# A hybrid decoder layer on one Trainium2 core: where the first weight sums of the projection are made, when their slices are loaded, and how often the activation table set is named

## The chip, the core and the metric

The kernel runs on one core of a Trainium2 chip. A core has TensorE (PE in the profile), VectorE (DVE), ScalarE (ACT), GpSimd (POOL) and SyncE (SP), whose queue issues nearly all transfers of this kernel, and 16 DMA engines. Each engine works through its own instructions in order and waits on semaphores for the others. The metric is the device time of one execution in microseconds (us); lower is better.

## The reference

One layer (DEPTH is 1) over 4096 tokens of width 1024:

```
mod = silu(c) @ ada_w + ada_b;  shift, scale, gate = split(mod, 3)
h = rms_norm(x, norm_pre) * (1 + scale) + shift
u = h @ w_in                                # (4096, 1024) @ (1024, 3720)
q, k, v, f_logit, z_rwkv, p_pool, g = split(u)
y_fox = forgetting attention, 8 heads of 64: q and k are RMS-normalised per head
y_rwkv = RWKV-7 recurrence, 4 heads of 64, over z_rwkv;  y_pool = causal pooling over p_pool
y = concat(y_fox, y_rwkv, y_pool) * silu(g)
out = x + gate * rms_norm(y @ w_out, norm_post)
```

The change touches only the way to u: the preparation (norms of the rows of w_in, shift and scale) and the projection h @ w_in.

## The kernel before, in words

The program is a row of blocks, `prepare`, `project`, `recur`, `attend` and `output`, with a barrier of all engines between one and the next. The change is in the first two.

**prepare** streams the eight row groups of w_in (128 x 3720 fp32 each, L143) and of the first 2048 columns of ada_w (L148) through SP's queue, in the order of the code: the four first loads, then w_in and ada_w by turns, each gated by the use of the slot it goes to. DVE takes the largest absolute value of each row of w_in (L257), and after the eighth makes its inverse `rinv` (L276). PE multiplies the ada_w slices by silu(c) (L221, 16 small matmuls a slice). Behind the w_in and ada_w loads SP issues eight loads of x (L165, the first 512 tokens in four tiles of two halves), and behind those the slices of w_in that the projection needs first: a wide one of 128 columns (L167) and a narrow one of 8 columns (L168, runs of 32 bytes) into slot 1 of `wraw`, and two of 128 columns (L171, `columns[0]`) into slot 0. ACT squares the x tiles and makes their inverse norms with Ln and Exp (L205 to L210); DVE scales the tiles (L248, `x_scaled`). A short chain of DVE (L279 to L285) makes a bound over all columns, POOL reduces it over the partitions (L194), and DVE makes the scales from it (L288 to L293). ACT names the table set that holds both Ln and Exp once here (L201).

**project** splits each fp32 operand into two fp16 pieces, high and low, and multiplies by a Strassen-like scheme with seven products of half-size blocks, so sums and differences of blocks have to be made of both operands. The token side runs over 4 super-blocks (`sb_`) of 1024 tokens, the weight side over 14 sets of 2 x 128 columns (`n`, `q` = n - 1 in super-block 0) and one single of 128 + 8 columns (n = 0). A step `g` is one of the 7 products of a set, or the single.

Before the loop over g stands a first phase, which makes the token side of super-block 0 in 16 units `u`: PE transposes (L676, `turn`), ACT brings the four blocks over (L722, L723), DVE makes four sums (L903 to L908), ACT rounds to the high pieces (L739), DVE subtracts for the low pieces (L915, `low`; semaphore `lo_made`). PE runs the single in four parts (`single(0, j)`, L652 and L659, L661), the j-th when 4(j + 1) units are low and `single_low` is done; in PE's order part j stands ahead of the transposes of unit 4(j + 2). DVE runs `single_low` (L926 to L931) at u = 6 and the low pieces of set 0 (L940 to L951) at u = 14 and 15. POOL begins with `single_weights` (L1117 to L1124: scale by rinv, high pieces, one difference), then `weight_sums(0)` (L1131 to L1143: scale 128 x 2048 by rinv, then four 128 x 512 differences), `first_high` (L1148 to L1151), and then the passes of `weight_sums(q)` for q = 1, 2, ... of the loop. SP loads the slices of set 1 (L507) when `single_low` is done, those of set 2 when the low pieces of set 0 are.

In the loop, a set of q or k columns needs per-head norms. For the x-th such tile: ACT squares it (L798), PE sums the squares with a matmul against `headmean` into the one bank `pss` (L684, `head_means`), ACT takes Ln of that bank (L804) and Exp (L806), DVE multiplies (L979, `normalise`), POOL rounds and stores. `head_means(x)` waits for the square of x and for the Ln of x - 1, since the bank is one; PE's next products are queued behind it. The square of x waits for `normalise(x - 2)`. There are 64 such tiles, 16 in a super-block, 4 in a set; the q and k sets are n = 7, 9, 11 and 13. Ahead of every Ln of L804 stands `preload_act_table_set(EXP_LN)` (L803), and so ahead of every Ln of `squares` (L748; 12 times, for the x tiles of the next super-block). The Sigmoid of the gate columns (L837, n = 1 to 4) is in another set.

## Time and profile before

| | us |
|---|---|
| three timed runs | 3635.66, 3657.88, 3661.07 |
| their median | 3657.88 |
| the profiled execution's own time | 3640.25 |
| its span in the trace | 3638.5 |
| PE busy in the span | 3315.0 (91%) |

The trace is of the execution of 3640.25 us, of which 1.75 us lie outside the span. Times in the rows below are counted from the span's start. `prepare` lasts until PE's first transposes at 82.4 us; the first phase of `project` from there to about 157 us; the loop of `project` to about 1430 us. A busy share of PE near 9 tenths or more means that whatever makes PE wait lengthens the time; idle time of the other engines costs only what it hands on to PE.

### The profile page before, as it was taken

What the parts mean: (1) busy time and instruction counts of PE and PEld (TensorE: products, weight loads), DVE (VectorE), ACT (ScalarE), POOL (GpSimd) and SP (SyncE); (2) the same over time, 40 slices, a digit from 0 to 9 for tenths busy, and PEclk for the clock granted to TensorE, in tenths of its full rate; (3) what the DMA queues carried; (4) which work ended last, traced back from release to release, by engine and by line L of the source; (5) the groups of instructions that cost most, each with busy time, mean ns of one, the idle gap of its engine ahead of it and who ended that gap; (6) DMA issues with size and microseconds to landing.
All of it is one profiled execution on the core that took longest, in us unless ns stands there. A gap on an engine that the chain in (4) does not pass through costs nothing. (4 is left out here: it accounts for less than half of the span.)

```text
span 3638.5 us, 90159 instructions
## 1 busy us (share of the span) xinstructions
PE 3315.0 (91%) x31941; PEld 2290.6 (63%) x31941; DVE 2435.1 (67%) x4320; ACT 2048.2 (56%) x3785; POOL 1793.2 (49%) x2071
## 2 busy tenths in 40 slices
PE   6597899999999997699999699999999999979998
PEld 6593369449647943588888366666666656645444
DVE  5797556434532333688784599889988988965554
ACT  2344654544543244577775477777777777753333
POOL 1477300330140042245553398889889889862222
PEclk9798999999999999799998699999999999989999
DMA  8297335334443533233221222020220211214555
GB/s 326 72 307 283 125 133 188 128 133 155 152 154 120 187 136 123 55 81 81 63 56 35 56 56 55 10 58 12 54 57 10 56 33 32 57 69 162 189 187 183
DMA packets 251932, 402.69 MB, mean 111 GB/s; under 512 B 86733, under 2 KB 203172, under 8 KB 236612
## 3 DMA queue, kind: packets, MB, share of 16 engines
q1 hardware_dynamic: 251019, 396.89, 34.6%
q8 instruction: 258, 4.23, 0.5%
q14 instruction: 175, 1.43, 0.1%
q0 software_dynamic: 480, 0.14, 0.1%
HBM read 274.38 MB, written 122.59 MB: 109 GB/s over the span
## 5 line engine op out<-in xcount | busy, mean ns | idle before, releaser
L2526 ACT ACTIVATE p<-psc,xb,sc 128x512 f32<-128x512 f32 (+3 forms) x1152 | 848.7, 744 | 318.4 <-PE psc L2617 305.7
L2504 POOL TENSOR_TENSOR plo<-p 128x512 f16<-128x512 f32 (+2 forms) x864 | 905.5, 1076 | 71.9 <-ACT p L2526 70.8
L2673 DVE TENSOR_REDUCE mx<-pm 128x1 f32<-128x512 f32 (+3 forms) x1201 | 732.0, 636 | 99.4 <-PE pm L2548 87.0
L627 PE MATMUL bank<-h,ring 128*128 128x512 f16 x2688 | 605.1, 384 | 5.4 <-DVE u L963 5.4
L2596 PE MATMUL po<-v,p 128*128 128x129 f16 x4224 | 513.3, 220 | 21.2 <-POOL plo L2504 18.0
L632 PE MATMUL bank<-ring,h 128*128 128x128 f16 x8064 | 465.7, 221 | 24.1 <-ACT c L791 12.3
L2598 PE MATMUL po<-v,plo 128*128 128x65 f16 x4224 | 483.7, 192 | 3.5 <-issue 3.5
L627 PEld LDWEIGHTS bank<-h,ring 128*128 128x128 f16 x2688 | 265.8, 99 | 350.5 <-issue 52.9
L632 PEld LDWEIGHTS bank<-ring,h 128*128 128x128 f16 x8064 | 462.9, 99 | 25.0 <-issue 12.6
L2596 PEld LDWEIGHTS po<-v,p 128*128 128x128 bf16 x4224 | 388.8, 97 | 123.7 <-POOL plo L2504 28.0
L1158 POOL CAST stage<-c 128x512 f16<-128x512 f32 x64 | 47.3, 740 | 814.1 <-DVE c L979 814.1
L2548 PE MATMUL pm<-ka,qa 128*128 128x512 f16 (+3 forms) x1201 | 438.4, 368 | 3.2 <-DVE mx L2673 2.8
L2598 PEld LDWEIGHTS po<-v,plo 128*128 128x128 f16 x4224 | 379.2, 98 | 95.9
L2615 PE MATMUL psc<-qa,ka 128*128 128x512 f16 (+3 forms) x1152 | 420.1, 365 | 0.0
L2617 PE MATMUL psc<-qb,kb 128*128 128x512 f16 (+3 forms) x1152 | 418.5, 363 | 0.0
L2889 PE MATMUL pz<-wo,yh 128*128 128x512 f16 x1024 | 305.9, 380 | 3.1 <-DVE yl L2921 3.1
L973 DVE TENSOR_TENSOR c<-bank,u 128x512 f32<-128x512 f32 x168 | 115.5, 688 | 249.6 <-PE bank L627 170.7
L2717 DVE TENSOR_TENSOR plo<-p 128x512 f16<-128x512 f32 (+1 forms) x288 | 281.6, 978 | 0.0
L2833 POOL TENSOR_TENSOR o<-o,xr 128x1024 f32<-128x1024 f32 x32 | 75.4, 2356 | 312.1 <-DVE o L2944 312.1
L2548 PEld LDWEIGHTS pm<-ka,qa 128*128 128x128 f16 x1201 | 118.6, 99 | 133.9 <-DVE mx L2673 14.6
L2889 PE MATMUL pz<-wo,yl 128*128 128x512 f16 x512 | 194.6, 380 | 0.0
L2889 PEld LDWEIGHTS pz<-wo,yh 128*128 128x128 f16 x1024 | 100.4, 98 | 117.7 <-issue 4.9
(405 smaller groups left out, 5662.3 us busy)
## 6 DMA issues: line engine op xcount, KB each, us to landing
ring<-scratch_ws SPq DMA_DIRECT2D x52, 1792.0 KB, 7.8
scratch_z<-stage SPq DMA_DIRECT2D x72, 256.0 KB, 2.8
scratch_ws<-h SPq DMA_DIRECT2D x10, 1792.0 KB, 8.1
y<-scratch_y SPq DMA_DIRECT2D x35, 512.0 KB
g<-scratch_g SPq DMA_DIRECT2D x35, 512.0 KB
xr<-in_x SPq DMA_DIRECT2D x34, 512.0 KB, 6.3
scratch_g<-stage SPq DMA_DIRECT2D x64, 256.0 KB, 5.9
scratch_qk<-stage SPq DMA_DIRECT2D x64, 256.0 KB, 2.6
```

The lines of the kernel that those rows point to most:

```text
L627: t = nc.tensor.matmul(bank[b][:], m.ring[:, slot, l, bo, k, :], hh[:, side, r, ao, k, :], start=fresh and first, stop=last, skip_group_ch ...
L632: t = nc.tensor.matmul(bank[b][:, ts], hh[:, side, l, ao, k, ts], m.ring[:, slot, r, bo, k, :], start=fresh and first and tp == 0, stop=la ...
L2504: nc.gpsimd.tensor_tensor(plo[:, k % NP, 0:w], p32[:, k % NP, 0:w], hi[:, 0:w], ALU.subtract)\
L2526: nc.scalar.activation(p32[:, k % NP, 0:w], psc[k % 2][:, 0:w], ACT.Exp, bias=xb[:, u, b, x // 4:x // 4 + 1], scale=m.sc[:, 0:1]).then_inc ...
L2548: ins = nc.tensor.matmul(pm[g][:, n, 0:w], qa[:, u, j * P:(j + 1) * P], ka[:, u, q * BT:q * BT + w], start=not last, stop=True, skip_group ...
L2596: nc.tensor.matmul(o[:, oc:oc + VW], hi[:, c0:c0 + P], v[:, u, x, 0:VW], start=(x == 0 and t % 2 == 0), stop=False, skip_group_check=True)
L2598: g = nc.tensor.matmul(o[:, oc:oc + 1 + HD], plo[:, k % NP, c0:c0 + P], v[:, u, x, 0:1 + HD], start=False, stop=(x == 4 * b + t), skip_gro ...
L2615: nc.tensor.matmul(psc[k % 2][:, 0:w], ka[:, u, ks], qa[:, u, t0:t0 + w], start=not diag, stop=False, skip_group_check=diag)
L2617: nc.tensor.matmul(psc[k % 2][:, 0:w], kb[:, u, ks], qb[:, u, t0:t0 + w], start=False, stop=True, skip_group_check=diag).then_inc(qk_mm.se ...
L2673: nc.vector.tensor_reduce(mx[:, s, t, q:q + 1], pm[g][:, 0, 0:w], AX.X, ALU.max).then_inc(pm_d.sem, 1)
L2717: tt(plo[:, k % NP, 0:w], p32[:, k % NP, 0:w], hi[:, 0:w], ALU.subtract).then_inc(lo_v.sem, 1)
L2889: mm = nc.tensor.matmul(pz[u % 2][j][:], l[:, u % 2, k // 4, ks], r[:, k, j * HALF:(j + 1) * HALF], start=(k == 0 and c == 0), stop=(k == ...
```

## The change

In `prepare`, SP issues the wide, the narrow and the two `columns[0]` slices right behind the first two pairs of w_in and ada_w, ahead of the loads with k = 2. POOL does there what `single_weights` and `weight_sums(0)` did in `project`: as soon as rinv is there (a new semaphore, `inverse`) it makes the single's scaled slice, its difference and its high pieces, then comes the reduction over partitions, then the scaling and the four differences of set 0. The difference of the single goes to a place of its own (`m.wtz`), and `wz` and `wf` live from `prepare` on. In `project`, POOL begins with `first_high`. Sets 0 and 1 now share one buffer of sums (`wt_of`), so the differences of set 1 wait until the low pieces of set 0 are made (`w_lo` of 2); `single_low` moves from u = 6 to u = 3, the low pieces of set 0 from u = 14 and 15 to u = 9 and 12. The table set is named ahead of L804 only at the first tile of each super-block, and in `squares` only from the third super-block on (`sb_ > 1`): 4 and 8 times in the code where it was 64 and 12.

```diff
--- before.py
+++ after.py
@@ -156,6 +156,13 @@
                 load_w(0)
                 load_ada(1)
                 load_w(1)
+                wide = slice(Z_COL + 6 * P, Z_COL + 7 * P)
+                sp.dma_start(m.wraw[:, 1, :, 0:P], a.w_in[0, :, wide].rearrange("(k p) c -> p k c", p=P)).then_inc(m.wraw_in[1], 16)
+                sp.dma_start(m.wraw[:, 1, :, P:P + FOX_HEADS], a.w_in[0, :, F_COL:F_COL + FOX_HEADS]
+                             .rearrange("(k p) c -> p k c", p=P), allow_slow_non_contiguous=True).then_inc(m.wraw_in[1], 16)
+                for side, c0 in enumerate(m.columns[0]):
+                    sp.dma_start(m.wraw[:, 0, :, side * P:(side + 1) * P], a.w_in[0, :, c0:c0 + P].rearrange("(k p) c -> p k c", p=P))\
+                        .then_inc(m.wraw_in[0], 16)
                 for k in range(2, KT):
                     load_w(k)
                     load_ada(k)
@@ -163,13 +170,6 @@
                     for half in range(2):
                         t0 = half * BT + j * P
                         sp.dma_start(m.x_first[j][:, half, :], a.x[0, t0:t0 + P, :]).then_inc(m.x_in[j], 16)
-                wide = slice(Z_COL + 6 * P, Z_COL + 7 * P)
-                sp.dma_start(m.wraw[:, 1, :, 0:P], a.w_in[0, :, wide].rearrange("(k p) c -> p k c", p=P)).then_inc(m.wraw_in[1], 16)
-                sp.dma_start(m.wraw[:, 1, :, P:P + FOX_HEADS], a.w_in[0, :, F_COL:F_COL + FOX_HEADS]
-                             .rearrange("(k p) c -> p k c", p=P), allow_slow_non_contiguous=True).then_inc(m.wraw_in[1], 16)
-                for side, c0 in enumerate(m.columns[0]):
-                    sp.dma_start(m.wraw[:, 0, :, side * P:(side + 1) * P], a.w_in[0, :, c0:c0 + P].rearrange("(k p) c -> p k c", p=P))\
-                        .then_inc(m.wraw_in[0], 16)
 
             @block.gpsimd
             def _(pool):
@@ -190,8 +190,31 @@
                 for k in range(ZC // P):
                     pool.dma_start(m.Z[k * P:(k + 1) * P, 0:m.HALO], zero[:]).then_inc(halo, 16)
 
+                tt, copy, wz, wf, wtz = nc.gpsimd.tensor_tensor, nc.gpsimd.tensor_copy, m.wz, m.wf, m.wtz
+                r, w = m.wraw[:, 1, :, :], P + FOX_HEADS
+                pool.wait_ge(m.wraw_in[1], 32)
+                pool.wait_ge(inverse, 1)
+                tt(r[:, :, 0:w], r[:, :, 0:w], m.rinv[:].unsqueeze(2).to_broadcast([P, KT, w]), ALU.mult).then_inc(wz_step, 1)
+                pool.wait_ge(wz_step, 1)
+                tt(wtz, r[:, 4:8, 0:w], r[:, 0:4, 0:w], ALU.subtract).then_inc(wz_step, 1)
+                copy(wz[:, 0, 0:2, :, :].rearrange("p o k c -> p (o k) c"), r[:, :, 0:P])
+                copy(wf[:, 0:2, :, 0:FOX_HEADS].rearrange("p o k c -> p (o k) c"), r[:, :, P:w])
+                pool.wait_ge(wz_step, 2)
+                copy(wz[:, 0, 2, :, :], wtz[:, :, 0:P])
+                copy(wf[:, 2, :, 0:FOX_HEADS], wtz[:, :, P:w])
                 pool.wait_ge(w_max, KT + 1)
                 nc.gpsimd.partition_all_reduce(bnd[:, 1:2], bnd[:, 0:1], P, RMAX).then_inc(allmax, 1)
+                r, t = m.wraw[:, 0, :, :], m.wt
+                pool.wait_ge(m.wraw_in[0], 32)
+                tt(r, r, m.rinv[:].unsqueeze(2).to_broadcast([P, KT, 2 * P]), ALU.mult).then_inc(wq_step, 1)
+                b11, b12, b21, b22 = r[:, 0:4, 0:P], r[:, 0:4, P:2 * P], r[:, 4:8, 0:P], r[:, 4:8, P:2 * P]
+                pool.wait_ge(wq_step, 1)
+                tt(t[:, 0, :, :], b12, b11, ALU.subtract).then_inc(wq_step, 1)
+                tt(t[:, 2, :, :], b22, b12, ALU.subtract).then_inc(wq_step, 1)
+                pool.wait_ge(wq_step, 2)
+                tt(t[:, 1, :, :], b22, t[:, 0, :, :], ALU.subtract).then_inc(wq_step, 1)
+                pool.wait_ge(wq_step, 4)
+                tt(t[:, 3, :, :], b21, t[:, 1, :, :], ALU.subtract).then_inc(wq_step, 1)
                 pool.wait_ge(halo, 16 * (ZC // P))
 
             @block.scalar
@@ -273,7 +296,7 @@
 
                 dve.wait_ge(w_max, KT)
                 chain(nc.vector.tensor_scalar(rowmax[:], rowmax[:], 1e-20, 1.0 / TW, ALU.max, ALU.mult))
-                chain(nc.vector.reciprocal(rinv[:], rowmax[:]))
+                nc.vector.reciprocal(rinv[:], rowmax[:]).then_inc(inverse, 1)
                 x_scaled(0)
                 dve.wait_ge(ada_mm, KT)
                 chain(nc.vector.tensor_tensor(m.ab[:], pcol[:, 0:2 * KT], m.cols[:, KT:3 * KT], ALU.add))
...
@@ -345,7 +367,6 @@
         hh = m.h
         wraw, wout = m.wraw, m.wout
         wts = [m.wt, m.xt[:].rearrange("p s d -> p (s d)").rearrange("p (o k c) -> p o k c", o=4, k=4)]
-        wtz = m.wt.rearrange("p o k c -> p (o k c)")[:, 0:4 * (P + FOX_HEADS)].rearrange("p (k c) -> p k c", k=4)
         early = c[:].rearrange("p n t -> p (n t)").rearrange("p (s o t) -> p s o t", s=2, o=8)
         acc = h7[:].rearrange("p s o t -> p (s o t)")[:, 0:DM]
         ones = h7[:].rearrange("p s o t -> p (s o t)")[:, DM:DM + P]
@@ -488,6 +509,9 @@
             if u >= 4:
                 eng.wait_ge(lo_made, u - (3 if u < 16 else 1))
 
+        def wt_of(q):
+            return wts[0] if q <= 0 or q % 2 else wts[1]
+
         def slot_of(q):
             return (m.ring if q < DIRECT else wout)[:, q % 2, :, :, :, :]
 
@@ -501,7 +525,7 @@
                     elif q == 2:
                         sp.wait_ge(w_lo, 2)
                     else:
-                        sp.wait_ge(w_sums, q)
+                        sp.wait_ge(w_sums, q - 2)
                         sp.wait_ge(w_lo_a, q - 2)
                     for side, c0 in enumerate(m.columns[q]):
                         sp.dma_start(wraw[:, q % 2, :, side * P:(side + 1) * P], a.w_in[0, :, c0:c0 + P].rearrange("(k p) c -> p k c", p=P))\
+                        nc.scalar.preload_act_table_set(EXP_LN)
                     activate(m.rstd[:, j, :], m.ssq[:, j, :], ACT.Ln, bias=m.eps[:, 0:1], scale=1.0 / DM).then_inc(std_x, 1)
                     act.wait_ge(std_x, nth_ + 1)
                     activate(m.rstd[:, j, :], m.rstd[:, j, :], ACT.Exp, scale=-0.5).then_inc(rstd_x, 1)
 
                 def weights_high_a(q):
 
-                    act.wait_ge(w_step, 1 + q * 4 + 1)
+                    act.wait_ge(w_step, 4 * (q - 1) + 1)
                     if 2 <= q < DIRECT:
                         act.wait_ge(mm, ended(0, q - 1, NP7 - 1))
                     if q == DIRECT:
@@ -765,8 +790,8 @@
 
                 def weights_high_b(q):
 
-                    act.wait_ge(w_sums, q + 2)
-                    activate(slot_of(q)[:, 0, 3:7, :, :], wts[(q + 1) % 2], ACT.Copy).then_inc(w_hi, 1)
+                    act.wait_ge(w_sums, q)
+                    activate(slot_of(q)[:, 0, 3:7, :, :], wt_of(q), ACT.Copy).then_inc(w_hi, 1)
 
                 def first_product(sb_, n):
 
@@ -800,7 +825,8 @@
                 def head_inverse(x):
 
                     act.wait_ge(ss_d, x + 1)
-                    nc.scalar.preload_act_table_set(EXP_LN)
+                    if x % 16 == 0:
+                        nc.scalar.preload_act_table_set(EXP_LN)
                     activate(sq[:, x % 2, :], pss[:], ACT.Ln, bias=m.eps[:, 0:1]).then_inc(ln_d, 1)
                     act.wait_ge(ln_d, x + 1)
                     activate(sq[:, x % 2, :], sq[:, x % 2, :], ACT.Exp, scale=-0.5).then_inc(rec_d, 1)
...
@@ -922,7 +948,6 @@
                 def single_low():
 
                     r = wraw[:, 1, :, :]
-                    dve.wait_ge(w_first_hi, 1)
                     tt(wz[:, 1, 0:2, :, :].rearrange("p o k c -> p (o k) c"), r[:, :, 0:P],
...
@@ -933,7 +958,7 @@
                 def weights_low_a(q):
 
                     if q == 0:
-                        dve.wait_ge(w_first_hi, 2)
+                        dve.wait_ge(w_first_hi, 1)
                     else:
                         dve.wait_ge(w_hi, 2 * q - 1)
                     h, o, r = slot_of(q)[:, 0], slot_of(q)[:, 1], wraw[:, q % 2, :, :]
@@ -948,7 +973,7 @@
                     if q >= 1:
                         dve.wait_ge(w_hi, 2 * q)
                     h, o = slot_of(q)[:, 0], slot_of(q)[:, 1]
-                    tt(o[:, 3:7, :, :], wts[(q + 1) % 2], h[:, 3:7, :, :], ALU.subtract).then_inc(w_lo, 1)
+                    tt(o[:, 3:7, :, :], wt_of(q), h[:, 3:7, :, :], ALU.subtract).then_inc(w_lo, 1)
 
                 def first_sum(sb_, n):
 
@@ -1041,13 +1066,13 @@
                 for u in range(18):
                     if u < 16:
                         sums(u)
-                    if u == 6:
+                    if u == 3:
                         single_low()
                     if u >= 2:
                         low(u - 2)
-                    if u == 14:
+                    if u == 9:
                         weights_low_a(0)
-                    if u == 15:
+                    if u == 12:
                         weights_low_b(0)
                 dve.wait_ge(fb_in, 16)
                 dve.wait_ge(carry0, 2)
@@ -1110,30 +1135,16 @@
                     ins.then_inc(pool_step, 1)
                     pool.wait_ge(pool_step, steps[0])
 
-                def single_weights():
-
-                    r, w, copy = wraw[:, 1, :, :], P + FOX_HEADS, nc.gpsimd.tensor_copy
-                    pool.wait_ge(m.wraw_in[1], 32)
-                    tt(r[:, :, 0:w], r[:, :, 0:w], m.rinv[:].unsqueeze(2).to_broadcast([P, KT, w]), ALU.mult).then_inc(w_step, 1)
-                    pool.wait_ge(w_step, 1)
-                    copy(wz[:, 0, 0:2, :, :].rearrange("p o k c -> p (o k) c"), r[:, :, 0:P])
-                    copy(wf[:, 0:2, :, 0:FOX_HEADS].rearrange("p o k c -> p (o k) c"), r[:, :, P:w])
-                    tt(wtz[:, :, 0:w], r[:, 4:8, 0:w], r[:, 0:4, 0:w], ALU.subtract).then_inc(w_sums, 1)
-                    pool.wait_ge(w_sums, 1)
-                    copy(wz[:, 0, 2, :, :], wtz[:, :, 0:P])
-                    copy(wf[:, 2, :, 0:FOX_HEADS], wtz[:, :, P:w]).then_inc(w_first_hi, 1)
-
                 def weight_sums(q):
 
-                    r, t = wraw[:, q % 2, :, :], wts[(q + 1) % 2]
-                    done = 1 + q * 4
+                    r, t = wraw[:, q % 2, :, :], wt_of(q)
+                    done = 4 * (q - 1)
                     pool.wait_ge(m.wraw_in[q % 2], 32 * (q // 2 + 1) + (32 if q % 2 else 0))
                     tt(r, r, m.rinv[:].unsqueeze(2).to_broadcast([P, KT, 2 * P]), ALU.mult).then_inc(w_step, 1)
                     b11, b12, b21, b22 = r[:, 0:4, 0:P], r[:, 0:4, P:2 * P], r[:, 4:8, 0:P], r[:, 4:8, P:2 * P]
                     pool.wait_ge(w_step, done + 1)
-                    if q:
-                        pool.wait_ge(w_lo, q)
-                    else:
+                    pool.wait_ge(w_lo, max(q, 2))
+                    if q == 2:
                         pool.wait_ge(tr_d, 4)
                     tt(t[:, 0, :, :], b12, b11, ALU.subtract).then_inc(w_step, 1)
                     tt(t[:, 2, :, :], b22, b12, ALU.subtract).then_inc(w_step, 1)
@@ -1147,8 +1158,7 @@
                     o, r, copy = m.ring[:, 0, 0, :, :, :], wraw[:, 0, :, :], nc.gpsimd.tensor_copy
                     copy(o[:, 0:2, :, :].rearrange("p o k c -> p (o k) c"), r[:, :, 0:P])
                     copy(o[:, 2, :, :], r[:, 4:8, P:2 * P])
-                    pool.wait_ge(w_sums, 2)
-                    copy(o[:, 3:7, :, :], wts[1]).then_inc(w_first_hi, 1)
+                    copy(o[:, 3:7, :, :], wts[0]).then_inc(w_first_hi, 1)
 
                 def pieces(sb_, n, half, side):
                     t, x = tile(sb_, n, half, side), nth(sb_, n, half, side)
@@ -1182,8 +1192,6 @@
                     step(tt(stage[hi, s, 0:BT], stage[hi, s, 0:BT], ps4[hi, m.HALO:E], ALU.add))
                     pool.sem_inc(ready[s], 1)
 
-                single_weights()
-                weight_sums(0)
                 first_high()
                 nc.gpsimd.memset(ph[:], 0.0).then_inc(p_clear, 1)
                 pool.wait_ge(p_clear, 1)
@@ -3001,6 +3009,8 @@
             m.h = weights.enter_context(nc.sbuf_tensor("h", [P, 2, 2, 7, 4, BT], F16))
             m.ring = weights.enter_context(nc.sbuf_tensor("ring", [P, 2, 2, 7, 4, P], F16))
             m.xt = weights.enter_context(nc.sbuf_tensor("xt", [P, 2, DM], F32))
+            m.wz = weights.enter_context(nc.sbuf_tensor("wz", [P, 2, 3, 4, P], F16))
+            m.wf = weights.enter_context(nc.sbuf_tensor("wf", [P, 3, 4, 2 * FOX_HEADS], F16))
             m.pscale = weights.enter_context(nc.sbuf_tensor("pscale", [P, 2], F32))
             m.rtab = weights.enter_context(nc.sbuf_tensor("rtab", [P, 2, m.HALO], F32))
             m.ssq = weights.enter_context(nc.sbuf_tensor("ssq", [P, 4, 2], F32))
@@ -3009,6 +3019,7 @@
             m.wraw = other[:, 0:4096].rearrange("p (s k c) -> p s k c", s=2, k=KT)
             m.wt = other[:, 4096:6144].rearrange("p (o k c) -> p o k c", o=4, k=4)
             m.wout = other[:, 6144:13312].bitcast(F16).rearrange("p (s l o k c) -> p s l o k c", s=2, l=2, o=7, k=4)
+            m.wtz = other[:, 12288:12288 + 4 * (P + FOX_HEADS)].rearrange("p (k c) -> p k c", k=4)
             m.x_first = [m.xt] + [other[:, 6144 + j * 2 * DM:6144 + (j + 1) * 2 * DM].rearrange("p (s d) -> p s d", s=2)
                                   for j in range(3)]
             prepare(nc, a, m)
```

## Rows read from the trace of the kernel before

**Rows 1.** The page, busy time, share of the span and instructions of each engine.

```profile
PE 3315.0 (91%) x31941; PEld 2290.6 (63%) x31941; DVE 2435.1 (67%) x4320; ACT 2048.2 (56%) x3785; POOL 1793.2 (49%) x2071
```

**Rows 2.** Windows: start:end, length, busy time per engine, PE clock, DMA share, GB/s.

```profile
0.00:82.40 82.40, 56.21 (x258) 55.43 (x258) 43.99 (x56) 13.63 (x27) 9.55 (x24) 1.00 0.93 360
82.40:157.00 74.60, 32.86 (x384) 29.41 (x384) 58.95 (x93) 29.82 (x50) 32.08 (x21) 0.70 0.11 29
```

**Rows 3.** Waits of PE, 156 to 1500 us: us in total, times, longest.

```profile
PE pss L684 <- ACT sq L804: 48.6, 28, 6.4
...
PE ptr L676 <- DVE xt L920: 7.9, 1, 7.9
```

**Rows 4.** The three lines that name the set: duration min/median/max in ns, first to last.

```profile
L803 ACT ACT_TABLE_LOAD  x64: 1283/1283/1283, 312.2 to 1414.6; - x64
...
L748 ACT ACT_TABLE_LOAD  x12: 1283/1283/1283, 358.1 to 951.1; - x12
...
L201 ACT ACT_TABLE_LOAD  x1: 1283/1283/1283, 4.8 to 4.8; - x1
```

**Rows 5.** Timeline in a late q or k set: start, us, operation [idle before <-releaser].

```profile
1405.91 0.72 ACT L798 ACTIVATE sq<-c,sc 128x512 f32<-128x512 f32 x1 [1.40 <-DVE c L979]
...
1406.65 1.28 ACT L803 ACT_TABLE_LOAD   x1
...
1407.94 0.69 ACT L804 ACTIVATE sq<-pss,eps 128x512 f32<-128x512 f32 x1
...
1408.78 1.10 PE L684 MATMUL pss<-sq,headmean 128*128 128x512 f32 x2 [0.90 <-ACT sq L804]
...
1413.52 1.10 PE L684 MATMUL pss<-sq,headmean 128*128 128x512 f32 x2 [1.06 <-ACT sq L804]
```

**Rows 6.** Timeline, other head waits of PE, and what ran around them.

```profile
432.44 1.10 PE L684 MATMUL pss<-sq,headmean 128*128 128x512 f32 x2 [0.90 <-ACT sq L804]
...
436.80 1.28 ACT L748 ACT_TABLE_LOAD   x1
...
441.26 2.05 PE L684 MATMUL pss<-sq,headmean 128*128 128x512 f32 x2 [5.13 <-ACT sq L804]
...
669.38 1.71 PE L684 MATMUL pss<-sq,headmean 128*128 128x512 f32 x2 [3.40 <-ACT sq L804]
...
670.88 3.88 PE L627 MATMUL bank<-h,ring 128*128 128x512 f16 x12
...
716.65 1.10 PE L684 MATMUL pss<-sq,headmean 128*128 128x512 f32 x2 [1.06 <-ACT sq L804]
```

**Rows 7.** Timeline at the end of the preparation.

```profile
58.66 14.12 PE L221 MATMUL pcol<-ccol,adaw 128*128 128x1 f32 x64 [0.48 <-DMA adaw<-in_ada_w]
...
63.01 9.76 SPq L168 DMA_DIRECT2D h<-in_w_in  x1
...
68.32 1.06 ACT L205 ACTIVATE sqp<-xt 128x1024 bf16<-128x1024 f32 x1 [62.25 <-DMA xt<-in_x]
...
74.31 0.38 POOL L194 PARTITION_ALL_REDUCE bnd<-bnd  x1 [64.23 <-DVE bnd L285]
...
79.59 1.42 DVE L248 TENSOR_SCALAR h<-h,rstd 128x1024 f32<-128x1024 f32 x2 [0.76 <-ACT rstd L210]
```

**Rows 8.** Timeline in the first phase of the projection.

```profile
96.92 3.68 DVE L903 TENSOR_TENSOR h<-h 128x128 f32<-128x128 f32 x1
...
118.58 3.60 POOL L1131 TENSOR_TENSOR h<-h,rinv 128x2048 f32<-128x2048 f32 x1 [8.41 <-DMA h<-in_w_in]
...
126.27 1.99 POOL L1143 TENSOR_TENSOR h<-h 128x512 f32<-128x512 f32 x1
...
130.99 1.08 DVE L915 TENSOR_TENSOR h<-h 128x896 f16<-128x896 f32 x1
...
132.92 1.08 DVE L915 TENSOR_TENSOR h<-h 128x896 f16<-128x896 f32 x1
...
150.96 4.44 PE L652 MATMUL bank<-h,wz 128*128 128x128 f16 x48 [4.79 <-DVE h L915]
```

More of the change, by code:

```diff
@@ L131, in prepare @@
         x_sq, x_std, x_rstd = sem("p_x_sq"), sem("p_x_std"), sem("p_x_rstd")
-        tab_made = sem("p_tab_made")
+        tab_made, inverse, wz_step, wq_step = sem("p_tab_made"), sem("p_inverse"), sem("p_wz_step"), sem("p_wq_step")
         zero = sb("zero", [P, m.HALO])
```

5 lines of the change are left out of this document (2 added, 3 removed).

## The prediction

> **What bounds the kernel now.** I read the page's first part, then windows by stage, then PE's own waits, then the timeline at the places those named. PE is busy 91% of the span [rows 1], so work taken off another engine counts only where PE waits for it. Two stretches are different: up to 82.4 us the DMA engines carry the time (share 0.93, 360 GB/s), and from 82.4 to 157 us PE is busy 32.86 of 74.60 us at a granted clock of 0.70, while DVE is busy 58.95 us [rows 2]. That first phase is bound by DVE, much of whose busy time is waiting for POOL, as shown below. In the loop of the projection the largest wait of PE is for the Ln of the head norms, 28 times, 48.6 us together, and one wait for scaled x adds 7.9 us [rows 3].
>
> **Part 1, the table set.** The three lines that name it give 64, 12 and 1 loads of 1283 ns each [rows 4]. The single naming in the preparation serves four tiles of Square, Ln and Exp (there is one load at L201, none beside it), so a set once there stays. The change leaves 4 of 64 and 8 of 12: 60 + 4 loads go, 64 x 1.283 = 82 us of ScalarE. What counts is their share of PE's waits. In a late set the square starts at 1405.91 and takes 0.72, the load follows at 1406.65, the Ln at 1407.94, and PE goes on at 1408.78 after 0.90 of idleness, and again at 1413.52 after 1.06 [rows 5]. The load stands in both chains, and it is longer than each wait, so each vanishes whole. Ten waits are of 0.90 (first 432.44, last 1408.78) and ten of 1.06 (first 716.65, last 1413.52) [rows 5, 6]: 9.0 + 10.6 = 19.6 us. The other eight make 48.6 - 19.6 = 29.0 us, from 2.10 to 6.39; each holds one removed load (1.28), and that of 5.13 at 441.26 also one of L748 at 436.80 [rows 6], where both go: 7 x 1.28 + 2.57 = 11.5 us. The wait for scaled x [rows 3] has one load of L748 ahead of it: 1.3 us. Sum 32.4 us. Could the chains meet a new stop at once? Behind the first wait of a set of q or k lies the same chain again (Exp, normalise, square, Ln), and it moves up by the same 1.28, so the second gain is not paid for by the first. Of the rest of each long wait, DVE's order of work is the cause, and it stays.
>
> After the waits of 3.40 and 5.13 the pss pair took 1.71 and 2.05, after the short ones 1.10, and behind the first twelve matmuls took 3.88 [rows 6]. PE had stood idle, and went on slower. If those twelve lose in the same ratio, such a place costs 0.61 + 3.88 x (1 - 1.10 / 1.71) = 2.0 us. With waits of 2.1 in place of 3.4 some of it may go; I take it for three places at half, 3 us (bounds 0 and 7). Table part: 35 us, bounds 28 and 40.
>
> The Trainium skill (ScalarE: Activation LUTs, What ACT_TABLE_LOAD costs) adds to the load a drain of about 1.38 us at a switch to a different set. By it the eight long waits would give 9 x 1.38 = 12 us more. The trace differs: the load starts 0.02 us after the square's end and the Ln right behind it [rows 5], so I leave it out of the sum.
>
> **Part 2, the preparation.** Four transfers move ahead of the k = 2 loads. They carry 0.52 + 0.03 + 1.05 = 1.6 MB, 4.5 us at 360 GB/s [rows 2]. SP was held 9.76 us at the narrow one, with a full queue in front [rows 7]; the same can happen now, and queued behind it are w_in 2, ada_w 2 and all that follows. While SP is held, the DMA engines have what fills the queue, so I count bytes and a little for the narrow runs: 5 us, bounds 3 and 10. Everything behind shifts: PE's eight passes over ada_w (14.12 for two, the last ending at 72.8), x (ACT begins its squares at 68.32) and the reduction over partitions at 74.31 [rows 7], now near 79.3. What the wait for bytes at the tail gives back is small, since the squares, not the trailing slices, ended the block.
>
> POOL's single part (one scaling, one difference, copies, some 5.5 us by width from the 3.60 of the 2048-wide scaling [rows 8]) fits between the inverse, near 72, and the reduction: hidden. The part of set 0 does not. A pass takes from 118.58 to 128.26, 9.7 us [rows 8], so it ends near 89.6. Meanwhile DVE has its three scales and six x_scaled halves (1.42 a pair [rows 7]) to do. Are they held up by POOL? A sum of 0.28 us became 3.68 while POOL scaled [rows 8]; these are other forms, so the bounds are 0 and all of them after POOL, 4.3 + 0.6 for the last small ones. I take half, 2 us: the block ends near 92 instead of 82.4, **9.6 us later**, bounds 6 and 15. The Trainium skill (SBUF — State Buffer, Who interferes with whom) says that a tensor_scalar in a two-port mode, and any operation with two inputs in SBUF, blocks against GpSimd for a whole instruction. By it I would take the upper end, 12 us. It speaks against doing this here.
>
> **Part 3, the first phase.** S is its start. Free of POOL a unit takes DVE 132.92 - 130.99 = 1.93 us [rows 8], about 0.93 for the sums and 1.0 for the low pieces. During a pass of POOL, 9.7 us, about one operation of DVE gets in at each of POOL's five boundaries (the 3.68 at 96.92 is one held until POOL's scaling ended), some 2.7 us of work; loss 7. Before, POOL's passes for sets 0 and 1 and the copies fall on DVE's way, single_low waits for POOL, and the last part of the single starts at 150.96, S + 68.6 [rows 8]. After, step by step: the copies of first_high hold DVE until S + 3.8; four units low with two sums ahead (9.6) and single_low between (1632 wide, by the 1.08 for 896 about 1.9) give S + 15. PE's first part takes 4.44 and its small matmuls (5.5, an estimate); the transposes for unit 8 are queued behind it, so with ACT's moves DVE has the next sums at S + 22.5. POOL's scaling for set 1 (its slices issued at S + 10, landing some 6 later by estimate) falls into this stall. Eight units are low at S + 26.3, the second part runs and holds unit 12 until S + 33.5, and DVE makes the low pieces of set 0 (3584 wide, 4 by the same rate) by S + 37.5. Now `w_lo` is 2, which frees POOL's four differences of set 1, 6 us, and SP's loads of set 2, which by the same 6 us land just as those end (near S + 44): a whole second pass follows without a gap, until S + 54. DVE has three groups of sums and five lows to do, 7.8 us, and is caught in both. Twelve units are low at S + 44, sixteen at S + 57.8, where the last part of the single starts. That is 92 + 57.8 = 149.8 against 150.96: **1.2 us sooner**. Bounds: 12 sooner (DVE slips more through POOL's gaps) and 12 later (preparation at its upper end, nothing slipping). The two thirds of POOL's work that left the first phase are paid for by the preparation, and the new wait on `w_lo` brings two passes together at the end of the chain. Later sets keep their order against PE.
>
> **The sum.** -35 - 1 = -36 us, from the profiled execution's own time 3640.25 (span 3638.5 and 1.75 outside): 3604. The median of the runs is 3657.88, and two of three lie near 3660, so the same change from there gives 3622. I can't tell on which level the middle run falls, and take 3614.
>
> **The rivals.**
> - The first phase gains and the preparation loses little: front -12, total -47, 3593 to 3611. For it: DVE's stalls on PE leave slack. Chance 0.12.
> - The preparation costs its upper end: front +12, total -24, 3616 to 3634. For it: the 9.76 us of SP and the 3.68 of a blocked sum. Chance 0.15.
> - The load was not what PE waited for, and normalise or the square's wait takes its place: only the pairs of 0.90 and 1.06 half, total -10, 3630 to 3648. Against it the timeline, in which Ln follows the load at once. Chance 0.05.
> - Slower than before: without the name ahead of each Ln, Ln and Exp are given sets of their own, two loads a tile in place of one. Then Exp, normalise and the next square come 1.28 later at all 28 waits: 28 x 1.28 = 36 us more, 3640 + 36 = 3676 (3694 from the median). It decides as soon as a load stands ahead of L806. Against it: one load at L201 for four pairs of Ln and Exp [rows 4]. Chance 0.03.
> - The skill's drain, by which a removed load frees 2.66: 12 us more than my sum, 3592 to 3610. The gap of 0.02 speaks against it. Chance 0.02.
>
> The forecast itself has 0.63, with its own range of 3597 to 3632.
>
> **How the numbers follow.** From 3590 (low level, front at its best) to 3642 (high level, front at its worst or a third of the table part lost) no more than 0.2 is left out. About 1% is what a measurement of this kernel can tell from no change, here 36.6 us, that is 3621. The forecast sits just on the good side when the middle run falls low and on the line when it falls high; with the better cases faster by over 1% gets 0.54, within 1% 0.43, slower by over 1% 0.03.
>
> **What would show it.** Right: L803 x4 and L748 x8; the row of PE waiting for L804 down to some 17 us in 8 waits, with none of 0.90 or 1.06; PE's first transposes near 92; the reduction near 79; L903 rows of several us only at S to S + 4, near S + 17 and from S + 37 on; the last start of L652 near 150. Wrong: loads in front of Exp; a new releaser in the place of L804; transposes past 97 (SP's queue starved the loads) or before 88; a last part of the single before 140 or after 160.

## The result, and the profile after

The changed kernel takes 3614.3 us in the median of 8 runs (3603.77 to 3624.66), the kernel before 3655.85 in 8 runs on the same chip (3635.66 to 3664.90). The ratio is 0.9891, with a 95% interval of 0.9866 to 0.9915: 41.5 us less by the medians. The interval does not reach 1, so the change is faster; whether by more than 1% it leaves open, since 0.9900 lies inside it. The forecast of 3614 met the time. Its two parts did not: the table part gave about 12 us more than forecast and the front took about 12 us more, and the two misses cancelled.

The page of the changed kernel, busy time of each engine (before: [rows 1]):

```profile
PE 3329.5 (92%) x31941; PEld 2311.4 (64%) x31941; DVE 2425.5 (67%) x4320; ACT 1963.3 (54%) x3721; POOL 1791.5 (49%) x2071
```

The two lines that name the set in the loop, by source line (columns as in [rows 4]):

```profile
L829 ACT ACT_TABLE_LOAD  x4: 1283/1283/1283, 324.0 to 1248.5; - x4
...
L773 ACT ACT_TABLE_LOAD  x8: 1283/1283/1283, 532.9 to 936.1; - x8
```

PE's waits between 156 and 1500 us (in total, times, longest, as in [rows 3]):

```profile
PE pss L708 <- ACT sq L830: 14.3, 8, 4.7
...
PE ptr L700 <- DVE xt L946: 6.7, 1, 6.7
```

ScalarE has 64 instructions less, exactly the loads, and 85 us less, of which the loads are 82. The wait for Ln [rows 3] fell from 48.6 us in 28 waits to 14.3 in 8. TensorE's matmuls are the same 31941.

The stages of the changed kernel, by windows (columns as in [rows 2]). The first two answer to the two of [rows 2]:

```profile
0.00:104.50 104.50, 56.22 (x257) 55.39 (x258) 44.19 (x56) 13.63 (x27) 24.25 (x35) 1.00 0.74 284
104.50:168.40 63.90, 34.55 (x384) 31.15 (x384) 54.82 (x93) 29.94 (x50) 23.66 (x14) 0.71 0.13 34
1392.00:2194.00 802.00, 705.33 (x6220) 580.05 (x6219) 575.04 (x1128) 516.07 (x1431) 393.24 (x469) 0.86 0.24 61
```

The preparation ends at 104.5 instead of 82.4 us and moves 284 GB/s instead of 360. The first phase, from there to the first product of the loop, is 10.7 us shorter. The third window is code that the change leaves alone. In the same stretch behind the projection the kernel before has this row:

```profile
1428.00:2230.00 802.00, 704.42 (x6495) 575.87 (x6495) 598.47 (x1166) 534.32 (x1460) 414.73 (x498) 0.89 0.24 61
```

PE is as busy in both, but finishes 6220 matmuls instead of 6495, at a granted clock of 0.86 instead of 0.89. What follows the projection takes 2231.3 us in the trace of after (3622.9 - 1391.6), 2211.1 in that of before and 2213.9 in that of the kernel with the table part alone (below, clock 0.90 in this stretch). The source there is the same in all three. So the spans of two single executions (3622.9 and 3638.5) understate the change. I therefore compare two things: medians, and **the end of the projection**, the first matmul behind its loop:

```profile
L733 PE MATMUL ptr<-h x4: 592/592/592, 1391.6 to 1392.9; 128*128 128x512 f32 x4
```

In before it starts at 1427.4. That is 35.8 us sooner, as the traces have it:

| kernel | first transposes | last part of the single | first product of the loop | end of the projection |
|---|---|---|---|---|
| before | 82.4 | 150.96 | 157.50 | 1427.4 |
| after | 104.5 | 161.93 | 168.91 | 1391.6 |
| tables_only | 82.3 | 150.86 | 157.44 | 1379.7 |
| front_only | 103.3 | 160.52 | 167.18 | 1437.0 |
| pe_reduce | 94.4 | 151.98 | 159.12 | 1382.0 |
| loads_early | 89.5 | 158.18 | 164.77 | 1434.7 |
| loads_late | 107.7 | 165.37 | 172.71 | 1395.9 |
| tables_pe_reduce | 82.3 | 148.34 | 154.73 | 1373.5 |
| own_sums | 95.6 | 148.58 | 156.00 | 1379.5 |
| single_sooner | 82.4 | 145.68 | 152.52 | 1375.0 |

These are single executions. Kernels with the same preparation differ by up to 1.2 us in its end (after and front_only, pe_reduce and own_sums), so a difference of about that size between two rows shows nothing.

From before to after the first product comes 11.4 us later, and from there to the end of the projection 47.2 us are gained. Two questions followed: why the tables give 47 and not 35, and where 22 us come from in a preparation that was to lose 9.6.

### The profile page after: what moved, and what is told of

It is laid out like the page before. It is cut to its first block and busy times, and to the rows that moved or that the text cites. A ratio compares the mean times of both kernels' runs of the same rounds, so it can differ in the third digit from the quotient of the medians.

```text
span 3622.9 us, 90094 instructions
## 1 busy us (share of the span) xinstructions
PE 3329.5 (92%) x31941; PEld 2311.4 (64%) x31941; DVE 2425.5 (67%) x4320; ACT 1963.3 (54%) x3721; POOL 1791.5 (49%) x2071
```

## The experiments

**1. The two parts apart.** tables_only is the kernel before with the two conditions on the table set and nothing else; front_only is the changed kernel with the set named each time.

```diff
+                    if sb_ > 1:
+                        nc.scalar.preload_act_table_set(EXP_LN)
...
+                    if x % 16 == 0:
+                        nc.scalar.preload_act_table_set(EXP_LN)
```

> The kernel before with nothing but the table set named less often (4 and 8 times instead of 64 and 12). Theory: the table part alone carries the gain, and the front part costs some 11 us. Then the preparation and the first phase stay as before (first transposes at 82.4, last part of the single at 151), each later super-block takes 301 us instead of 310, and the projection's last matmuls start near 1380 instead of 1427: 47 us less, ratio 0.987, and some 11 us faster than the changed kernel. Rival: the first super-block's extra gain (18 us where 10 were forecast) comes from GpSimd being ahead with the weight sums; then the last matmuls start near 1388 and the ratio is 0.990.

> The changed kernel with the table set named as often as before (64 and 12 times), so only the front part is left. Theory: 11 us slower than before, ratio 1.003; first transposes at 104.5, last part of the single at 162, the 28 waits of PE for the Ln of the head norms there as before with 48 us, last matmuls of the projection near 1439. Rival: the sums that are made ahead shorten the first super-block by some 8 us; then they start near 1431 and the time is within 3 us of before.

Measured: tables_only 3608.09 us (5 runs) against 3652.79 (17 runs of before), ratio 0.9873 (0.9842 to 0.9903), end of the projection 47.7 sooner. front_only 3665.88 (12 runs), ratio 1.0040 (1.0019 to 1.0060), end of the projection 9.6 later. So the tables carry the whole gain, and the front is a small loss. (The intervals of after and tables_only overlap; that tables_only is the better of the two rests on the front's own loss in front_only and on the end of the projection, 11.9 sooner.) The rival that POOL's work, now done sooner, helps the first super-block fell: that super-block is 18.3 us shorter with the tables alone (from the first product to the start of the second super-block, 364.64 to 346.35), and 18.0 in after.

**2. Who makes the reduction over partitions.** In after POOL stands still around it. The timeline of the changed kernel at the end of the preparation:

```profile
80.48 0.21 POOL L204 CAST wf<-h 128x32 f16<-128x32 f32 x1
...
81.38 0.16 DVE L308 TENSOR_TENSOR bnd<-bnd 128x1 f32<-128x1 f32 x1
...
86.35 0.38 POOL L206 PARTITION_ALL_REDUCE bnd<-bnd  x1 [5.66 <-issue]
...
88.13 4.07 DVE L271 TENSOR_SCALAR h<-h,rstd 128x1024 f32<-128x1024 f32 x6
...
93.64 3.59 POOL L209 TENSOR_TENSOR h<-h,rinv 128x2048 f32<-128x2048 f32 x1 [6.91 <-issue]
...
101.09 1.26 POOL L217 TENSOR_TENSOR h<-h 128x512 f32<-128x512 f32 x1
...
104.53 1.94 PE L700 MATMUL ptr<-ident,xt 128*128 128x128 f32 x8 [24.54 <-PEq L74]
```

POOL is free at 80.69 and its input is there at 81.54, but the reduction starts at 86.35. The next scaling, whose slices landed long before, starts 6.91 behind it. In neither gap does the profile show anything that POOL waits for. The gap ahead of the reduction is counted from POOL's last operation and not from the input: in loads_late (experiment 3) the bound is ready at 74.30, 9 us before POOL's last copy ends, and the gap behind that copy is 5.58 all the same. pe_reduce takes the reduction from POOL: PE turns the bounds into a row, DVE takes the maximum, PE spreads it over the partitions.

```diff
-                pool.wait_ge(w_max, KT + 1)
-                nc.gpsimd.partition_all_reduce(bnd[:, 1:2], bnd[:, 0:1], P, RMAX).then_inc(allmax, 1)
+                pe.wait_ge(w_max, KT + 1)
+                nc.tensor.transpose(prow[0:1, :], bnd[:, 0:1], m.ident[:]).then_inc(allmax, 1)
+                pe.wait_ge(allmax, 2)
+                nc.tensor.matmul(pall[:, 0:1], mrow[0:1, 0:P], mrow[0:1, P:P + 1], start=True, stop=True).then_inc(allmax, 1)
...
+                nc.vector.tensor_reduce(mrow[0:1, P:P + 1], prow[0:1, :], AX.X, ALU.max).then_inc(allmax, 1)
```

> The changed kernel, with the maximum over the partitions made by a transpose on PE, a maximum on DVE and a one-row matmul instead of partition_all_reduce on GpSimd. Theory: the idle 5.7 us ahead of that operation and 6.9 us behind it are the price of GpSimd changing over to other code and back, and both lie on the way to the end of the preparation. Then GpSimd goes on with set 0 at 81 to 82 without a gap, the first transposes start at 93 instead of 104.5, and the time is 11 us below the changed kernel: ratio to before 0.986. Rival: the gaps are waits for the bound and for DVE's scaling; then set 0 starts after 86 and the gain is under 3 us.

> The kernel before with the tables of the change and with the reduction on PE, nothing moved. In the kernel before GpSimd stood idle for 15 us between the reduction and the single's weights, 7.3 of them after the barrier. Theory: that too is the change of code; GpSimd starts at 82.5 instead of 89.7, the single's weights and the first low pieces come 7 us sooner, the last part of the single starts near 144 instead of 151, and the time is 7 us below tables_only, near 0.985. Rival: the first phase is held by DVE alone, and an earlier GpSimd only moves its collisions; then it is within 2 us of tables_only.

Measured: pe_reduce 3609.39 us (6 runs), ratio 0.9872 (0.9839 to 0.9904). Its first transposes start at 94.4 instead of 104.5, and the projection ends 9.6 sooner than in after. Its timeline:

```profile
78.44 0.67 POOL L206 CAST wf<-h 128x32 f16<-128x32 f32 x1
79.08 4.09 POOL L209 TENSOR_TENSOR h<-h,rinv 128x2048 f32<-128x2048 f32 x1
...
79.83 3.36 DVE L308 SCALAR_TENSOR_TENSOR gcol<-ab,cols 128x8 f32<-128x8 f32 x1
...
85.81 0.37 PE L248 MATMUL prow<-ident,bnd 128*1 128x128 f32 x1 [6.23 <-DVE bnd L313]
...
94.38 1.94 PE L707 MATMUL ptr<-ident,xt 128*128 128x128 f32 x8 [7.24 <-PEq L74]
```

Both gaps are gone: the scaling follows the copy at once. What the gaps had covered now shows. A sum of eight columns (L308) takes 3.36 us, until POOL's scaling is done, where the like one (L303) took 0.31 in after. With the next sums it brings the bound to 85.76 instead of 81.54. POOL's pass is over at 88.30, and the preparation now ends with DVE's six halves of x and four small scales, at 93.51: DVE is last where POOL was. That is why 11.7 us of lateness removed (4.8 ahead of the reduction, 6.9 behind it) gave 10.1, and 8.9 in own_sums, whose preparation is the same (95.6). The first scale of DVE is taken from `pall`, the reduction's new place.

The kernel before has such a gap too: its first scaling in the projection, in the timeline, is

```profile
89.74 1.99 POOL L1117 TENSOR_TENSOR h<-h,rinv 128x1088 f32<-128x1088 f32 x1 [15.05 <-issue]
```

It starts 7.3 us after the engines have met at 82.4. tables_pe_reduce (tables_only with the reduction on PE) removes it, with the slices loaded as before, so the gap was no wait for them. Its timeline:

```profile
82.33 2.01 POOL L1126 TENSOR_TENSOR h<-h,rinv 128x1088 f32<-128x1088 f32 x1 [72.25 <-POOLq L74]
...
148.34 4.28 PE L659 MATMUL bank<-h,wz 128*128 128x128 f16 x48 [3.67 <-DVE h L924]
```

POOL starts 7.4 sooner, but the last part of the single only 2.5 sooner (148.34 against 150.86). That DVE meets the same work of POOL elsewhere is my reading; no run takes it apart. The end of the projection is 6.2 sooner than in tables_only, 3.5 of it gained behind the first product: PE's two rows of waiting for DVE's u add 10.4 and 4.0 us there, 11.9 and 5.5 in tables_only. The time is 3600.16 us (5 runs), ratio 0.9863 (0.9831 to 0.9894), the lowest median of all. Both expectations, that the work moves up by the length of the gap, held for POOL, and only in part for PE.

**3. The place of the loads.** loads_early is the kernel before with the four slice loads moved ahead of the loads with k = 2, and nothing else. loads_late is the changed kernel with them back behind the loads of x.

```diff
@@ loads_late, on the changed kernel
-                wide = slice(Z_COL + 6 * P, Z_COL + 7 * P)
...
                 for k in range(2, KT):
                     load_w(k)
                     load_ada(k)
...
+                wide = slice(Z_COL + 6 * P, Z_COL + 7 * P)
```

> The kernel before, with only the four slices loaded amid w_in as in the changed kernel. Theory: the place of the loads alone puts ada_w, w_in and x 7 us later, since SP stands at the narrow slice (11 us in the changed kernel) with the k = 2 loads queued behind it. Then PE's last pass over ada_w ends at 80 instead of 72.8, the first transposes start near 89.6, the last part of the single near 158, and the time is 7 us above before, ratio 1.002. Rival: the bytes alone count, 4.5 us at 360 GB/s, and what trails at the end before is saved; then the transposes start at 85 to 87.

> The changed kernel, with the four slices loaded behind x as before. Theory: GpSimd's work in the preparation then waits for them: single's weights from 78, the reduction at 90, set 0 from 97 to 106, first transposes near 108 although PE's passes over ada_w end at 72.8 again. Some 3 to 4 us slower than the changed kernel, ratio 0.990. Rival: the 7 us that the loads cost come back whole; then the transposes start at 98.

Measured: loads_early 3661.03 us (10 runs) against 3656.23 (17 runs of before), ratio 1.0017 (0.9993 to 1.0040). Its first transposes start at 89.5 and its projection ends at 1434.7, 7.1 and 7.3 later. By the times alone it can't be told from before (the interval holds 1); the 7 us are the traces'. loads_late 3621.94 (4 runs), ratio 0.9911 (0.9888 to 0.9934); first transposes at 107.7, end of the projection 1395.9, 4.3 later than in after. The timeline of the changed kernel shows how it comes:

```profile
5.79 11.27 SPq L161 DMA_DIRECT2D h<-in_w_in  x1
17.10 6.59 SPq L164 DMA_DIRECT2D h<-in_w_in  x2
...
24.36 0.61 SPq L148 DMA_DIRECT2D adaw<-in_ada_w  x1
...
35.64 6.99 PE L244 MATMUL pcol<-ccol,adaw 128*128 128x1 f32 x32 [10.78 <-DMA adaw<-in_ada_w]
...
73.00 6.99 PE L244 MATMUL pcol<-ccol,adaw 128*128 128x1 f32 x32 [0.65 <-DMA adaw<-in_ada_w]
```

SP is held 17.9 us by the slices, so the load of ada_w 2 is issued only at 24.36. In before it is issued at 17.63, when its slot comes free, so 6.7 of the 17.9 delay it. PE, which multiplies ada_w as it comes, stands 10.78 us (4.46 in before), and its last pass ends at 80.0 instead of 72.8. That is 7.2 us. So the early place costs 7.2 by itself, and loads_early shows it (7.1) without any of POOL's part. In loads_late that price is gone (PE's last pass ends at 72.9), but POOL's part for the single stands ahead of the reduction in its queue and waits for slices that are now the last to land, so the reduction itself comes at 89.04 instead of 86.35. The timeline of loads_late:

```profile
89.04 0.38 POOL L206 PARTITION_ALL_REDUCE bnd<-bnd  x1 [5.58 <-issue]
...
96.84 3.59 POOL L209 TENSOR_TENSOR h<-h,rinv 128x2048 f32<-128x2048 f32 x1 [7.42 <-issue]
```

Given that POOL's work stays in the preparation, the early place was the better one by the traces; the intervals of the two times overlap. Two more gaps of 5.58 and 7.42 us stand around the reduction here.

**4. Can the moved work be made to pay?** own_sums is pe_reduce with a buffer of its own for the sums of set 1, so that POOL need not wait for the low pieces of set 0. single_sooner is tables_pe_reduce with `single_low` at u = 3.

```diff
@@ own_sums, on pe_reduce
+            return m.wt1 if q == 1 else wts[0] if q <= 0 or q % 2 else wts[1]
...
-                    pool.wait_ge(w_lo, max(q, 2))
+                    if q == 1:
+                        pool.wait_ge(tr_d, 8)
+                    else:
+                        pool.wait_ge(w_lo, q)
@@ single_sooner, on tables_pe_reduce
-                    if u == 6:
+                    if u == 3:
```

> pe_reduce, and the sums of set 1 go to a place of their own (the space of the first x tile behind xt), so GpSimd's differences for set 1 wait for eight transposes instead of the low pieces of set 0. Theory: that wait is what brings two passes of GpSimd together at the end of the first phase, where VectorE is the chain; without it the pass for set 1 runs at once behind its scaling, at 110 to 120, half of it while VectorE waits for PE anyway, and the last part of the single starts at 144 to 147 instead of 152. Ratio 0.985. Rival: VectorE loses the same at either place; then it stays at 151 to 153.

> tables_pe_reduce, and VectorE makes the single's low pieces at u = 3 instead of u = 6. GpSimd has the single's high pieces ready at 88 there, so nothing waits. Theory: the first part of the single starts when four units are low, near 105 instead of 110, SP's loads of set 1 start sooner by as much, and the last part of the single starts near 145 instead of 148.3: 3 us below tables_pe_reduce. Rival: the collisions with GpSimd only move, and the last part stays within 1 us.

Measured: own_sums 3604.71 us (6 runs), ratio 0.9864 (0.9838 to 0.9891). single_sooner 3603.28 (5 runs), ratio 0.9865 (0.9845 to 0.9886). The last part of the single starts at 148.58 in own_sums, 53.0 behind the first transposes instead of 57.6: the wait on `w_lo` had cost 4.6 us. The projection ends 2.5 sooner; of the rest, 1.2 is the later end of the preparation in this execution. In single_sooner it starts at 145.68, 2.7 sooner as expected, and the projection still ends 1.5 later than without the move: PE's two rows of waiting for DVE's u add 12.0 and 5.4 us in place of 10.4 and 4.0. Those rows are 11.9 and 5.5 in tables_only too, so it is tables_pe_reduce that has them short, and why is open. By the end of the projection no move of the front beats the tables with the reduction on PE. By their times tables_only, pe_reduce, tables_pe_reduce, own_sums and single_sooner (0.9863 to 0.9873) can't be told apart.

## Why the prediction was right, and what in it was wrong

**The table part: mechanism right, size low (35 forecast, 47.7 measured).** PE's waits for Ln, square and scaled x, 60.0 us together in before (48.6 + 3.5 + 7.9), are 22.3 in tables_only (14.8 + 0.8 + 6.7). That is 37.7 where I had 32.4. Nineteen of the twenty waits of 0.90 and 1.06 vanished; that of 0.90 at 432.44 became 0.65 (at 422.77). The eight long ones gave 14.9 where I had 11.5, since two chains held two loads where I counted one: in the first super-block 3.40 became 0.69 (at 381.06, then 377.43), and 2.56 vanished. 5.13 became 2.42, two loads as I had counted. A wait of 3.52 for the square, which I had at nothing, became 0.85.

```profile
377.43 1.10 PE L684 MATMUL pss<-sq,headmean 128*128 128x512 f32 x2 [0.69 <-ACT sq L806]
...
1355.57 1.02 PE L684 MATMUL pss<-sq,headmean 128*128 128x512 f32 x2
...
1359.02 1.02 PE L684 MATMUL pss<-sq,headmean 128*128 128x512 f32 x2
```

This is the timeline of tables_only, at that place and in a late set. It also shows a part of the remaining 10.0 us. From one pss pair to the next it is 3.45 us where no wait is left. With a wait of 1.06 in [rows 5] it was 4.74, that is 1.29 more: a short wait costs some 0.23 us beyond its idle time. Over the nineteen that went this makes 4.3.

The larger part is the slow restart, a term I had at 3 us. At five places of before, behind waits of 3.52 (422.69), 5.13 (441.26), 2.56 (484.50) and twice 3.40 (669.38 and 979.77), the step from the start of the pss pair to that of the next group is 1.7, 1.6, 1.7, 1.5 and 1.5 us longer than at the same place of tables_only, 7.9 together. One of them, in the timeline of before:

```profile
979.77 1.49 PE L684 MATMUL pss<-sq,headmean 128*128 128x512 f32 x2 [3.40 <-ACT sq L804]
...
981.05 4.09 PE L627 MATMUL bank<-h,ring 128*128 128x512 f16 x12
```

And the place at 669.38, in the timeline of the changed kernel, where the twelve matmuls now take 2.75 us:

```profile
662.39 1.10 PE L708 MATMUL pss<-sq,headmean 128*128 128x512 f32 x2 [1.98 <-ACT sq L830]
```

What fell at such a place is the granted clock. The windows of before (columns as in [rows 2]), the first two at 484.50 and the last at 381.06:

```profile
484.50:490.10 5.60, 5.60 (x18) 2.40 (x19) 0.75 (x1) 4.66 (x7) 1.77 (x2) 0.70 0.26 89
486.40:488.40 2.00, 2.00 (x6) 0.66 (x5) 0.00 (x0) 1.98 (x3) 1.24 (x2) 0.50 0.00 0
381.00:385.00 4.00, 3.94 (x18) 1.97 (x18) 2.19 (x6) 1.55 (x3) 0.55 (x1) 1.00 0.00 0
```

It fell to 0.50, the lower of its two levels (1.2 GHz), for part of the stretch; over the five places it is 0.67 to 0.70, and at all five it is 1.00 in tables_only. The length of the wait alone does not decide it: behind the 3.40 at 381.06 the clock stayed at 1.00 and the twelve took 2.75. I had taken the restart at three places and at half, since the wait would remain; the runs show five, and that behind what is left of the waits (1.97 and 2.42) PE goes on at full pace. 7.9 and 4.3 make 12.2; the stretches between, which I did not trace one by one, take 2.2 of it back.

**The preparation: 9.6 forecast, 22.1 measured; the step that failed is the set-0 pass.** I let it follow the reduction at once. By the forecast's own chain: the bound was ready 2.2 us later than I had it (the loads cost 7.2, not 5, though within their bounds of 3 and 10), the reduction started 4.8 late, and the scaling 6.9 behind it; the pass itself was 1.0 shorter, and the rest 0.4. Together 12.5, which is the miss. In that rest two errors cancel: from the end of POOL's pass (102.35) to the first transposes it took 2.15 us, near the 2.4 that I had, but not for the reason I gave, since DVE was done 9.6 us before that end. In the three traces in which POOL is last (after, front_only, loads_late) this step is 2.15, where DVE is last some 0.9. The two gaps were not among my bounds, and 22.1 lies outside 6 to 15. The trace of before had the row: POOL stood 15.05 us before its first scaling, and only half of that was the meeting of the engines. I had read POOL's rows from 118 us on and not the first. The Trainium skill (GPSIMD Engine Reference, Instruction dispatch) tells of a load of about 6 us on the first call to a freshly loaded kernel, with no instruction in the profile; the size and the invisible gap agree with 5.66 (after, front_only) and 5.58 (loads_late) ahead of the reduction. It says nothing of a second price on the way back, 6.91, 7.58, 7.42 and 7.3 here.

**DVE blocked by POOL: my 2 us were not paid in after, but the mechanism is there.** The six halves of x took 4.07 us while POOL stood in its gap. Without the gap, in pe_reduce, a small sum was held 3.36. The rule that I weighed against the change (the Trainium skill, SBUF — State Buffer, Who interferes with whom) agrees with that row. Its price was hidden by a larger one.

**The loads.** The sign that I had named, transposes past 97 because SP's queue starved the loads, came in (104.5), and loads_early shows the queue's share of it: 7.1.

**The first phase: right, and closely.** Forecast 57.8 us from the first transposes to the last part of the single; it was 57.4. The steps stand in the timeline of the changed kernel, with the start S at 104.5:

```profile
121.30 3.69 DVE L929 TENSOR_TENSOR c<-c 128x128 f32<-128x128 f32 x1
...
142.50 1.38 POOL L1149 TENSOR_TENSOR h<-h 128x512 f32<-128x512 f32 x1 [17.66 <-DVE ring L976]
...
148.45 3.65 POOL L1143 TENSOR_TENSOR h<-h,rinv 128x2048 f32<-128x2048 f32 x1
148.56 3.69 DVE L930 TENSOR_TENSOR c<-c 128x128 f32<-128x128 f32 x1
...
161.93 4.87 PE L676 MATMUL bank<-h,wz 128*128 128x128 f16 x48 [8.45 <-DVE h L941]
```

DVE is caught once at S + 17; POOL waits for the low pieces of set 0 until S + 38; the loads of set 2 land just as its differences end, and a whole second pass follows from S + 44. Where I wrote that the two thirds of POOL's work that left are paid for by the preparation, the sign was right: the phase gained 11.2 us and the preparation lost 22.1. With the preparation at 22.1 that still gave a loss and not the gain of 1.2.

**The rivals.** That the front gains fell (it lost 11). The rival of +12 for the front came nearest to its 11.0, though not by its own working: it had the preparation at its upper end of 15, and that took 22.1. Its total of -24 fell with the tables. Three others fell: that the load was not what PE waited for, that Ln and Exp get sets of their own (no load stands ahead of Exp: 4 and 8 loads in all), and a drain at each load. The last needs a word, since 47.7 is near the 47 that it gave. The rule of the Trainium skill (ScalarE: Activation LUTs, What ACT_TABLE_LOAD costs) is for a switch to a different set, and the removed loads named the set that was there, since no other load came in their place. Whole waits vanished at late sets for one load and nothing more: 1.29 from pair to pair is the wait and its restart, and a drain of 1.38 ahead of a load is nowhere in the timeline. It does not show at a real switch either. L863 is the Sigmoid of the gate columns, L773 names the set of Ln and Exp, and they come by turns in the timeline of the changed kernel:

```profile
532.65 0.19 ACT L770 ACTIVATION_READ_ACCUMULATOR sqx<-xt 128x1 f32 x1
532.86 1.28 ACT L773 ACT_TABLE_LOAD   x1
534.16 0.29 ACT L774 ACTIVATE rstd<-ssq,eps 128x2 f32<-128x2 f32 x1
...
534.59 0.58 ACT L809 ACTIVATE c<-bank 128x512 f32<-128x512 f32 x1
535.19 1.28 ACT L863 ACT_TABLE_LOAD   x1
```

Both loads start 0.02 us behind the instruction before them. The likeness of the sums is chance.

**The sum.** -1.2 became +11.0 at the last part of the single and +11.4 at the first product, -35 became -47. The end of the projection is 35.8 sooner against a forecast of 36. The time was met by two errors of opposite sign, so it says nothing for the working of either. A third pair is in it: 3614 was 36 below 3650, halfway between two levels, and the median of before came out at 3655.85, with a change of 41.5 by the medians. The 5.5 between 36 and 41.5 is within the interval of the ratio, so it is luck too. Left alone, either would have taken the forecast off by 12 us. front_only, whose first product is 9.7 late and whose projection ends 9.6 late, says the same of the front as 11.4 in after does; the 1.2 between their first transposes (103.3 and 104.5) stands between two executions of the same preparation: in front_only POOL has its inverse 1.9 sooner, and its gap behind the reduction is 7.58 instead of 6.91. I made no run to explain either.

## What to carry to other kernels

A table set that is named each time is loaded each time, even where it is loaded already; name it where the set really changes, and count each vanished wait of TensorE with its restart, and a long one with the granted clock behind it. Before work is put beside a library operation of GpSimd, look for idle rows put down to nothing right before and right behind it, in the old trace: each change of direction cost 5.6 to 7.6 us here, and a plain transpose and a matmul on TensorE did the same reduction without them. A transfer cut into many small runs, issued ahead of the bulk loads, holds the queue that issues it, and what it delays is whatever stands behind it in that queue.

## What the runs showed of the hardware that was not expected

- GpSimd stands still on both sides of `partition_all_reduce`, with its inputs ready and nothing shown: 5.66 and 6.91 us in after, 5.66 and 7.58 in front_only, 5.58 and 7.42 in loads_late, 7.3 behind it in before. With the reduction on TensorE the scaling at 79.08 follows the copy at once. That it is code being changed is a reading, supported by the 6 us of the Trainium skill (GPSIMD Engine Reference, Instruction dispatch) for one direction; the runs show only that the gap goes with the operation.
- A short wait of TensorE costs 0.23 us more than its idle row: 4.74 us from pair to pair with a wait of 1.06, and 3.45 without, at a granted clock of 1.00.
- After two waits of 3.40 us twelve matmuls of 128x512 took 3.88 and 4.09 us at a granted clock of 0.67, and after one of 2.56 us 4.43 at 0.70; after a third of 3.40, at 381.06, and after 1.98 they took 2.75 at 1.00.
- The four slice loads held SP for 17.9 us early in the queue (11.27 at the narrow one), where the 1.6 MB they move would take 4.5 at 360 GB/s.
- The granted clock behind the projection was 0.86 in one execution and 0.89 and 0.90 in two others with the same code there, and the one at 0.86 took 17 to 20 us more for all that follows the projection: nearly half of the whole change.
